# A two-layer mixture-of-experts backbone: layer two's residual rows kept on chip, expert results added by one-hot products instead of scatter DMAs

## The reference

```python
for l in range(DEPTH):
    need_ctx = l < DEPTH - 1
    ...
    hx = _rmsnorm(x, norm1[l]) * (1.0 + sc1) + sh1
    hc = _rmsnorm(ctx, norm1[l]) * (1.0 + csc1) + csh1
    ox, oc = _mixer(hx, hc, ...)
    x = x + g1 * ox
    hx2 = _rmsnorm(x, norm2[l]) * (1.0 + sc2) + sh2
    x = x + g2 * _ec_moe(hx2, router[l], w_gate[l], w_up[l], w_down[l])
    ...
return _rmsnorm(x, norm_final)

def _ec_moe(h, router, w_gate, w_up, w_down):
    cap = CAPACITY_FACTOR * n // N_EXPERTS
    aff = jax.nn.softmax((h @ router).astype(jnp.float32), axis=-1)
    g, idx = lax.top_k(jnp.swapaxes(aff, 1, 2), cap)
    xs = h[bidx, idx]
    a = jnp.einsum('becd,edf->becf', xs, w_gate)
    u = jnp.einsum('becd,edf->becf', xs, w_up)
    y = jnp.einsum('becf,efd->becd', jax.nn.silu(a) * u, w_down) * g[..., None].astype(h.dtype)
    return jnp.zeros_like(h).at[bidx, idx].add(y)
```

## Time and profile before

| | us |
|---|---|
| median of three runs | 2023.76 |
| lowest, highest | 2019.76, 2034.69 |
| profiled execution | 2019.55 |
| its span, first to last instruction | 2017.4 |
| PE busy | 1783.5 (88%) |
| DVE, ACT, POOL busy | 565.3, 353.4, 258.5 |

### The profile page before, as it was taken

One profiled execution on the slowest core, in us unless ns is written; L12 is line 12 of the kernel. 1 busy time (PEld: TensorE's weight loads), 2 busy tenths in 40 slices (PEclk: granted clock), 3 DMA queues, 4 the chain that ended last, 5 costly groups with the idle time before them and its releaser, 6 DMA issues.

```text
span 2017.4 us, 31015 instructions
## 1 busy us (share of the span) xinstructions
PE 1783.5 (88%) x13434; PEld 922.1 (46%) x13434; DVE 565.3 (28%) x1272; ACT 353.4 (18%) x768; POOL 258.5 (13%) x368
## 2 busy tenths in 40 slices
PE   6999899899969999999999699999948977777774
PEld 3867346774424444444443587558523322222221
DVE  2322455662441111111111332566241110110101
ACT  3200334562210000000000311446220000000001
POOL 1000223000011111121210100320000110101100
PEclk8999999999979999999999799999978999999998
DMA  9257422006359999999998700000678999999997
GB/s 387 108 211 275 181 105 84 2 1 261 141 219 393 394 395 394 397 394 395 395 397 327 266 22 1 1 1 2 250 301 328 395 395 401 403 402 398 405 404 302
DMA packets 85937, 531.06 MB, mean 263 GB/s; under 512 B 11568, under 2 KB 13872, under 8 KB 27184
## 3 DMA queue, kind: packets, MB, share of 16 engines
q1 hardware_dynamic: 67680, 486.13, 60.1%
q0 software_dynamic: 15920, 42.74, 7.5%
q10 hardware_dynamic: 2208, 0.26, 0.1%
HBM read 506.03 MB, written 23.07 MB: 262 GB/s over the span
## 4 chain that ended last, share of the span: by engine, by line
PE 71%; DMA 21%; DVE 4%; ACT 3%; issue 1%; SPq 0%; POOL 0%; DVEq 0%; ACTq 0%; POOLq 0%
PE psum L1351 16%; PE psum L1354 8%; DMA ring<-in_w_down 7%; PE psum L1240 7%; PE psum L1056 6%; PE psum L1345 6%; PE psum L1016 6%; DMA ring<-in_w_gate 5%; PE psum L1137 5%; PE psum L1110 5%; DMA arena<-in_w_down 4%; PE psum L1162 2%; PE psum L1191 2%; PE psum L966 2%; ACT arena L864 2%; DMA arena<-in_w_gate 1%
## 5 line engine op out<-in xcount | busy, mean ns | idle before, releaser
L1351 PE MATMUL psum<-ring,arena 128*32 128x512 f32 x1984 | 258.8, 593 | 1.1 <-DVE arena L1831 1.1
L1345 PE MATMUL psum<-ring,arena 128*64 128x512 f32 x888 | 214.7, 617 | 49.5 <-DMA ring<-in_w_gate 25.0
L1345 PE MATMUL psum<-arena 128*64 128x512 f32 x648 | 155.9, 611 | 41.0 <-DMA arena<-in_w_gate 20.2
L930 ACT ACTIVATE arena<-psum 128x768 f32<-128x768 f32 (+1 forms) x32 | 22.5, 704 | 956.5 <-PE psum L1354 463.4
L1354 PE MATMUL psum<-ring,arena 128*32 128x256 f32 x1984 | 152.6, 379 | 0.0
L1843 DVE SCALAR_TENSOR_TENSOR arena<-psum,gcur,arena 128x512 f32<-128x512 f32 x32 | 24.0, 751 | 443.1 <-PE psum L1354 228.4
L1345 PEld LDWEIGHTS psum<-ring,arena 128*64 128x64 f32 x888 | 59.0, 139 | 189.7 <-issue 106.1
L1240 PE MATMUL psum<-ring,arena 128*128 128x512 f32 x320 | 142.5, 597 | 0.0
L864 ACT ACTIVATE arena<-psum,smx 128x768 f32<-128x768 f32 (+4 forms) x160 | 118.8, 748 | 122.4 <-DVE smx L1594 122.4
L673 POOL TENSOR_SCALAR arena<-arena,smx 128x768 f32<-128x768 f32 (+1 forms) x40 | 77.9, 1947 | 447.4 <-DVE smx L1659 447.4
L1354 PEld LDWEIGHTS psum<-ring,arena 128*32 128x32 f32 x1984 | 64.6, 110 | 148.3 <-issue 148.3
(11 more groups left out here) (249 smaller groups left out, 1865.8 us busy)
## 6 DMA issues: line engine op xcount, KB each, us to landing
ring<-in_w_gate SPq DMA_DIRECT2D x84, 1024.0 KB, 28.2
ring<-in_w_up SPq DMA_DIRECT2D x80, 1024.0 KB, 28.7
ring<-in_w_down SPq DMA_DIRECT2D x79, 1024.0 KB, 29.4
arena<-in_w_down SPq DMA_DIRECT2D x49, 1024.0 KB, 28.2
ring<-in_w_ada SPq DMA_DIRECT2D x48, 1024.0 KB, 6.3
arena<-in_w_up SPq DMA_DIRECT2D x48, 1024.0 KB, 28.5
arena<-in_w_gate SPq DMA_DIRECT2D x44, 1024.0 KB, 29.3
ring<-in_w_in SPq DMA_DIRECT2D x18, 1024.0 KB, 25.2
```

Source lines behind the costliest of these rows:

```text
L1345: ins = mm(psum[64 * n:64 * n + 64, b * 512:(b + 1) * 512], lhs(k), w[:, n * 512:(n + 1) * 512], start=k == 0, stop=k == KD - 1)
L1351: ins = mm(psum[r0:r0 + 32, b * 512:(b + 1) * 512], lhs(k)[:, 32 * g:32 * g + 32], w[:, n * 512:(n + 1) * 512], start=k == 0, stop=k == KD ...
```

## The change

1. In layer two the four row blocks stay in the arena (held, at 8192 on), from the output projection to the end. They take the place of two LATE slots, so layer two has 19 slots instead of 21. The stores of res and the loads at the end go away, and with them the waits of the LATE slots on stores and transposes.
2. In layer two no scatter is issued. DVE builds from the token numbers (a row of 0 to 511 on each partition) a matrix "onehot" with the gate value where the token's number stands, PE multiplies it with the expert's result into psum (to_tokens: two parts of two token blocks, four products each), and DVE adds the psum to the held rows (summed). Part 0 of an expert stands in the middle of the next expert's UP product, part 1 behind it.
3. POOL's loop in layer two only gathers.
4. The end adds the last expert's sums block by block (final_sum) and norms from the held rows.
5. D steps have their values in bank 7 (3584), save for layer one's first 16 steps, and turn waits for "mix" only there.

```diff
-    EXTRA = [LATE, [BIG + 10240, BIG + 12288, BIG + 14336] + LATE]
+    EXTRA = [LATE, [BIG + 10240, BIG + 12288, BIG + 14336] + LATE[0:4]]
...
     def values_at(st):
-        return 2816 if st.kind == "D" else 3584
+        return 2816 if st.beside_ada else 3584
...
                     if m == RING + EARLY[l]:
                         sp.wait_ge(free, spent(where[("wout", l)]) + 4)
-                        sp.wait_ge(*LS[l]("ot", nq(l)))
...
+                        if l < DEPTH - 1:
+                            sp.wait_ge(*LS[l]("ot", nq(l)))
...
-        sp.wait_ge(*LS[DEPTH - 1]("sc", 16 * NE))
-        for t in range(NX):
-            sp.dma_start(f_x[t], res[toks(t), :]).then_inc(f_in[t], 16)
...
-                if st.i >= 2 and (st.kind == "D" or steps[st.i - 1].kind == "D"):
+                if st.kind == "D" and st.i >= 2 and steps[2 * (st.i // 2) - 1].beside_ada:
                     pe.wait_ge(*L("mix", st.i // 2))
...
+                pool.wait_ge(*L("lg", nq(l)))
+                pool.dma_start(modrow[:], numbers.broadcast_to([P, SEQ])).then_inc(s_num, 16)
...
+            def to_tokens(e, part):
+
+                pe.wait_ge(*L("yg", e + 1))
+                if part == 0 or e < NE - 1:
+                    pe.wait_ge(*L("ad", 2 * e + part))
+                for blk in (2 * part, 2 * part + 1):
+                    for h in range(2):
+                        half = slice(64 * h, 64 * h + 64)
+                        ins = mm(bank(sums_at(part, blk, h, e)), onehot[half, blk * P:(blk + 1) * P], yg[l][half, 0:512],
+                                 start=True, stop=True)
+                ins.then_inc(L["sa"], 1)
...
+            def summed(e, part):
+                dve.wait_ge(*L("sa", e * 2 + (part + 2)))
+                for blk in (2 * part, 2 * part + 1):
+                    for h in range(2):
+                        half = held[blk][:, 512 * h:512 * h + 512]
+                        ins = tt(half, half, bank(sums_at(part, blk, h)), ALU.add)
+                ins.then_inc(L["ad"], 1)
...
             for e, par in body_experts(dve):
-                if not (isinstance(e, int) and e == 0):
+                first_one = isinstance(e, int) and e == 0
+                if not first_one:
                     rows_out(e - 1, unit_no(l, e, DOWN + 4 - UNITS_E))
                 rows_in(e + 1, 1 - par)
+                if last and not first_one:
+                    summed(e - 1, 0)
                 gated(e, unit_no(l, e, UP + 4))
+                if last and not first_one:
+                    summed(e - 1, 1)
                 hidden_out(e)
```

More of the change, by code:

```diff
@@ L149, in build_program @@
     o_t = area(BIG + 9216, D)
-    f_x = o_x + [o_t]
+    held = [area(8192 + D * t, D) for t in range(NX)]
+    h_n = [area(BIG + 9216 - D * n, D) for n in range(2)]
     MOE1 = BIG + 5120
+    onehot = area(BIG + 4608, NX * P)
+    spare = [area(MOE1 + 1536, D), area(MOE1, D)]
     xg = [area(BIG + 10240, D), area(MOE1 + 1536, D)]
@@ L492, in lam_init, with row_x, row_n, sums_at @@
         return 0.8 - 0.6 * math.exp(-0.3 * l)
+    def row_x(l, t):
+        return held[t] if l == DEPTH - 1 else o_x[t % 3]
+    def row_n(l, t):
+        return h_n[t % 2] if l == DEPTH - 1 else o_n[t % 2]
+    def sums_at(part, blk, h, e=None):
+        return (0, 2, 4, 6)[2 * (blk % 2) + h] if part and e == NE - 1 else 1 + 4 * (blk % 2) + 2 * h
     def rows_landed(l, t):
@@ L1405, in _ @@
             if last:
+                mm(bank(0, NE), ident[:], sel[:], start=True, stop=True).then_inc(L["sa"], 1)
                 turn_rows(0)
@@ L1425, in _ @@
                     turn_rows(e + 1)
-                    product(e, UP, 4, latent_in(par), context_in(par))
+                    with_sums = last and e
+                    product(e, UP, 4, latent_in(par), context_in(par),
+                            (lambda e: to_tokens(e - 1, 0)) if with_sums else None)
+                    if with_sums:
+                        to_tokens(e - 1, 1)
                 pe.wait_ge(*L("xs", e + 2))
@@ L1770, in _ @@
                 dve.wait_ge(*L(f"ox{t % 3}", 16 * (t // 3 + 1)))
-                dlink(dve, tt(o_t, bank(2 * (t % 2), D), g1row[s], ALU.mult))
-                tt(o_x[t % 3], o_x[t % 3], o_t, ALU.add).then_inc(L["x1"], 1)
+                if last and t >= 2:
+                    dve.wait_ge(*L("ot", t - 1))
+                    dve.wait_ge(*L(f"stn{t % 2}", 16 * (t // 2)))
+                part = row_n(l, t) if last else o_t
+                dlink(dve, tt(part, bank(2 * (t % 2), D), g1row[s], ALU.mult))
+                tt(row_x(l, t), row_x(l, t), part, ALU.add).then_inc(L["x1"], 1)
                 if t == NX:
@@ L1824, in gated @@
             def gated(e, units_done):
+                if last and isinstance(e, int) and e == 0:
+                    dve.wait_ge(*L("stn1", 16 * len(range(1, nq(l), 2))))
                 dve.wait_ge(free, units_done)
```

124 lines of the change are left out of this document (91 added, 33 removed).

## The result

The changed kernel takes 2009.32 us (median of 8 runs, 2002.2 to 2013.24) against 2026.51 (8 runs, 2019.76 to 2034.69): ratio 0.991, 95% interval 0.9886 to 0.9934, so 13 to 23 us faster. The forecast was 1996 and a gain of 25 us. The range, 1982 to 2017, holds the result, the direction is right, the gain was some 8 us smaller than forecast.

What follows compares the result with a forecast made beforehand. Layer two's experts were taken as bound by the DMA weight stream, with PE waiting. Terms -20.3 + 5.0 - 4.4 + 1.6 - 2.1 - 5.0 = -25.2 took 2019.55 us to 1994.3; with 1.7 allowed, forecast 1996, range 1982 to 2017.

Steps and rivals of the forecast that it cites:

- Part 1: Layer two's expert weight stream: fifteen scatters left out free 1.35 us each of DMA time, -20.3 us.
- Part 2: Start of layer two's weight stream: two slots fewer cost +5.0 us; the first gather's chain comes earlier, -4.4 us.
- Part 3: PE in layer two's experts: one-hot products add 3.5 us per expert, 25.6 in total, hidden behind the stream's 31.3.
- Part 4: VectorE in layer two's experts: the adds are hidden except in the last expert, where DOWN ends +1.6 us later.
- Part 5: Tail after the last product: 17.9 us instead of 20.0, so -2.1 us, bounds -5 and +1.
- Part 6: Attention's differential steps: values in their own bank remove PE's waits for VectorE's copy, -5.0 us.
- Rival C: Stream gains, but the early chain doesn't: gather still 8.4 us, attention waits return as exponent waits; 2003 us, chance 0.22.

Runs made afterwards that it cites:

- run 4: Kernel before without layer two's scatters, so the experts' results are not added: 2006.34 us against 2030.34, ratio 0.9868.
- run 5: Kernel before with 19 slots instead of 21 for layer two's weights, row stores and their waits kept: 2028.81 us against 2030.34, ratio 1.0004.
- run 6: Changed kernel without the one-hot products and adds of experts 0 to 14, only the last expert's kept: 2001.94 us against 2030.34, ratio 0.9854.
- run 2: Kernel before with only the differential values moved to bank 7: 2020.81 us against 2026.12, ratio 0.9969; the reverse, changed kernel with bank 5 and its waits back: 0.9913.
- run 3: Changed kernel with one removed wait on "mix" put back, in the first window step behind the differential steps, both layers: 2006.37 us.

## Why the prediction was right, and where it was off

| step | forecast | measured | from |
|---|---|---|---|
| Part 1, scatters | -20.3 | -18.0 | run 4 |
| Part 2, two slots | +5.0 | +4.3 | run 5 |
| Part 2, first gather | -4.4 | -3.8 | start, 106.0 to 102.2 |
| Parts 3 and 4, one-hot work | +1.6 | +5.0 | run 6 |
| Part 5, tail | -2.1 | -2.9 | 20.0 to 17.1 |
| Part 6, bank | -5.0 | -1.7 | run 2 |
| sum | -25.2 | -17.1 | |

The measured terms come from kernels with one part each and need not add up exactly: the three terms of the stream, -18.0, +4.3 and +5.0, give -8.7, where the stream of the changed kernel is 7.3 us shorter than the mean of 473.0. The two profiles without many disturbances differ by 16.0, the medians by 17.2. The errors of the slots and the tail, 0.7 and 0.8 us to the good, hid a part of the others.

**What bounds the kernel** was read rightly from the earlier trace rows: full DMA engines with PE at 7 to 8 tenths. Everything that loads PE and VectorE there was nearly hidden, and everything that came off the DMA engines came off the time.

**Part 1** was a tenth too large. Of its two prices, 1.42 us by the engines' time and 1.24 us by bytes, the second was the better one; what came back is 1.2 us each. Why not all of the engines' time came back isn't shown.

**Part 2** held in both halves, and with the right link between them: taking slots away and letting the gather through early are the same act. The DMA engines were empty when the gather came, and it landed in 3.9 us. That the late slots are issued without the pause adds nothing that can be seen: run 5 keeps it and has the same "start" (101.7 and 102.2).

**Part 3** held. 1.92 us per group instead of 1.74 says that the halves of 64 rows do overlap; one after the other would be 3.5. The Trainium skill (TensorEngine Tiling (Array Packing), Key Properties) says that a change of tiling mode drains TensorE. The group of four stands between products of another tile shape, and its excess over two pairs of the earlier trace rows is 0.18 us. An expert has four such changes more than before, and its whole excess, 26.3 to 25.6, is 0.7 us. So the trace shows at most some 0.2 us for a change, which was put at nothing and is hidden here; whether a drain takes it isn't shown.

**Part 4** is the first step that failed: +1.6 us was forecast, 5.0 measured. The chain that it priced, from the gating product to DOWN's first unit, is right (5.1 us forecast, 5.05 measured). Three things beside it were put at nothing. The gating product itself starts 1.1 us later (run 6): 0.5 us by the weights, which land that much later, and 0.6 us by the one-hot group that stands in the middle of UP. The last expert of before was a poor measure: its stretch from the gating product to the end of DOWN, 10.5 us, holds waits for weights that scatters had held up, and without scatters it is 9.9 (runs 4 and 6), which makes 0.6. And behind the 2.60 us wait PE ran part of DOWN at half clock: 5.35 us against 3.65, so DOWN took 8.8 where 7.0 was forecast, 1.7 us. 1.6 + 1.1 + 0.6 + 1.7 is 5.0. The drop of the clock stands in both profiles of the changed kernel and in run 3's, but not in the one with the bank back, where the same wait of 2.60 is followed by 3.65. There the stretch from the gating product to the end is 12.1 us, just as forecast. So the drop is likely there, not bound to be.

**Part 5** was a little pessimistic: two adds took 1.27 us, not 1.38, and squares and scalings overlapped better. The tail of before is 20.6 to 20.9 in three other profiles, so the gain may be nearer to 3.5.

**Part 6** is the second step that failed. "I take -5.0, bounds -6.5 and -2" named the return of waits for exponents, and that was the smaller part of what came. In layer two the waits left as counted (4.1 us in the differential steps, 3.8 in the earlier trace rows), and then a stretch at 1.2 GHz took 1.5 back. In layer one 2.2 us of the waits left instead of 2.7, 0.7 came back as waits for exponents, and the stretch at 1.2 GHz took more than what was left (+0.9 in place of -2.7). The sum was 1.7 us, below the forecast's lower bound. Rival C ("the early chain doesn't gain") was half true: its attention part came, for the most part by another mechanism, its gather part did not.

**The base.** The forecast started from the one profiled execution, 2019.55, and allowed 1.7 us to the median. The median of eight runs of before is 7.0 us above that execution. Of the 13 us between 1996 and 2009.3 this is 5.3; the 8.0 us between the gains, 25.2 and 17.2, is the rest.

## What to carry to other kernels

When the DMA engines are full and PE and VectorE are not, work that trades a DMA for a product is nearly free until the last piece: in the last expert the stream no longer covers it, so there put what the next product needs ahead of the work that can wait. Price slots in a prefetch window together with whatever small transfer queues behind them, since the two can cancel to nothing. And when the difference is under 1%, compare stage lengths between fixed marks in the trace, in more than one profile: their sum repeated to 0.1 us in two profiles of the changed kernel whose spans differed by 6, and to 2.5 us in three of the kernel before.

## What the runs showed of the hardware that was not expected

- Removing PE's waits on "mix" in layer two was followed by a lower granted clock at the same place in every profile (0.83 to 0.91 in 1360 to 1370, six of six), and putting one wait back in the first window step restored 1.00 (two of two) and gained 1.4 us. In layer one the same wait put back did not (0.81 in 355 to 375, one profile).
- A pause of PE of 2.60 us was followed by half clock in three of four profiles (5.24 to 5.35 us for 16 instructions) and not in the fourth (3.65).
- Stretches at half clock also come and go in code that did not change (16 instructions at 29.8 us: 2.45 or 3.56 us); two profiles of the changed kernel differ by 6 us through them. The eight runs of before spread over 15 us, those of the changed kernel over 11.
- An accumulating scatter of 0.26 MB took 1.42 us of the 16 engines where a gather of 0.26 MB took 0.88, and leaving it out gave 1.2 us back.
